# A gated-delta recursion, the samples' delta step and branch A's gates and state update as one stage behind the solve

## The chip, the cores and the metric

One core of one Trainium2 chip runs the whole kernel. The metric is the device time of one execution in microseconds (us), the median of the runs shown. The core has five engines with a program each: PE (matrix products), DVE (vector), ACT (scalar functions), POOL (GpSimd) and SP, which here only issues transfers. They wait for each other on semaphores.

## The reference, cut to what matters

The kernel is one step of a hybrid decoder layer for 512 prompt tokens and 8 sample tokens (one new token for each of 8 requests, each with a stored state): two token mixers on one input projection, then a retrieval of experts (PEER). The change touches mixer A only, the gated DeltaNet with 4 heads of 128 x 128 state:

```python
# prompt, chunked; T = inverse of (I + L) of each chunk; the kernel uses chunks of 128, so 4 of them
u = T @ (v * beta);  w = T @ (k * beta * exp(G))
def step(S, xs):                       # one chunk after the other
    v_new = u_c - w_c @ S
    o     = qg_c @ S + qk_c @ v_new
    S     = S * g_c + kd_c.T @ v_new
    return S, o
# samples: S_t = a (I - b k k^T) S_{t-1} + b k v^T,  o = S_t^T q    (a chunk of length 1)
o_a = rmsnorm(o_a, gn_a) * silu(gate_a)      # per head, for prompt and samples
```

The outputs of this part are the gated `o_a`, the last prompt state `delta_p` and the eight new sample states `delta_s`.

## The kernel before

The program is a row of stages. Each is a function under `@phase` (L166): it issues one block of five engine programs, and at its end all engines meet in a barrier (L173) before the next stage begins. A stage's SP program waits for its own transfers before that barrier. Within a stage the order of work on each engine is written out by hand; there is no planner.

Around the change the stages are these, in this order.

**convolve** (L788): the short convolution of the 12 channel tiles on DVE (L893 and L895), SiLU on ACT (L916), then the sums of squares for the L2 norm (ACT L926 squares, PE L855 products with a column of ones), then the transposes that make `k_tok` and `v_tok`.

**delta_prompt** (L945): it prepares the decay matrices, inverts the four triangular matrices by seven levels of doubling (L1018 to L1171; `n` counts the 28 pairs of level and chunk), and then, in the same block, does the rest for the prompt. PE makes `u` and `w` for each chunk (L1054 and L1055) into banks 2 and 3, ACT copies them to `X` and `LT` (L1111 and L1113), and PE waits for these copies before the next chunk. DVE multiplies `k_tok` by the decay (L1174). Then comes the recursion: for each chunk, PE makes `w S` (L1064), DVE subtracts it from `u` (L1180), PE makes the output and the state's increment interleaved (L1071 to L1073), and DVE scales `S` and adds the increment (L1183 and L1184); PE's next chunk waits for that. SP stores `delta_p` (L984).

**delta_sample** (L1269): SP loads the samples' states (four transfers of 512 KB, L1294), POOL clears `kq`, DVE fills it, PE multiplies all 32 old states by their keys and queries (L1348, 64 passes), and DVE works out the samples' new values and outputs in six operations of 8 x 512 (L1327 to L1333).

**gate_and_turn** (L1355): for the five token tiles (four of 128, one of 8), ACT squares and sums per head and takes the root (L1414 and L1417), DVE scales and gates (`scale`, L1387 and L1390), PE transposes (L1446), ACT writes the upper part (`upper`, L1421), DVE the rest (`lower`, L1397). Between them runs the update of the eight sample states (`StateUpdate`, L1191): for a sample, ACT masks the stacked keys (L1208), PE makes the outer products of four heads (L1218) into one of two banks, DVE adds them to the decayed states (L1229, four instructions). SP stores the states in pairs (L1238). `Stack` (L1243) makes the stacked rows: POOL clears, ACT copies twice, DVE subtracts (L1265).

A second thread of work runs through the stages. **Side** (L577) projects 24 column tiles of `w_in` for later use, a few in each stage, as filling for PE. A tile is loaded by SP (L601), rounded by ACT (L647), split by POOL (L621), multiplied by PE in two halves of 24 passes each (L635 to L637), taken out by ACT (`take`, L664) and stored by SP (L613). `SIDE_BESIDE` (L74) says how many tiles go beside which stage: 7 in convolve ("cv"), 10 in delta_prompt ("dp"), 1 in delta_sample ("ds"). In convolve, PE's program does all halves first and the sums of squares behind them; ACT takes a result after each channel tile's SiLU, and the squares follow after the last take.

Behind these stages come branch B's projection ("proj_b", whose first chunk of weights is loaded early into `raw0`), rotation, retention, the merge, the output projection, and the experts, which take more than half of the time.

The program that calls the stages (L2111) allocates `masks` and `conv_st` before the projection of A, and the states of the samples after delta_prompt.

## Time and profile before

| | us |
|---|---|
| median of 3 runs | 2331.44 (2331.11 to 2332.11) |
| the profiled execution | 2330.46 |
| its span in the trace | 2328.7 |
| PE busy over the span | 1856.2 (80%) |
| DVE busy | 1302.1 (56%) |
| ACT busy | 890.2 (38%) |
| POOL busy | 644.1 (28%) |
| granted TensorE clock, mean | 0.944 of full |

The span is measured from the first to the last recorded instruction; 1.8 us of the execution's time lie around it. Times in the rows are from the span's start. A busy PE is not PE at its peak, since products are pipelined. The shares are means over stages with different limits, so what a change in one stage is worth is read in that stage.

### The profile page before, as it was taken

To read this page: it belongs to the slowest core of one execution; us is meant where nothing else is said; L and a number is where in the kernel's file an instruction comes from. 1 tells how busy PE (TensorE), PEld (TensorE's weight loads), DVE (VectorE), ACT (ScalarE), POOL (GpSimd) and SP (SyncE) were. 2 spreads that over 40 slices of the span, in tenths; PEclk is the share of its full clock that TensorE was granted. 3 is DMA by queue.
4 is the path that set the end of the run, shared out by engine and by line. 5 is a ranking of instruction groups with operands and counts; after the bars stand their busy time and mean duration, and the time that the engine had idled before them with its cause. 6 is when DMAs were issued, how large, how long until landed. Compare 5 with 4: busy or idle time off the path is not lost.

```text
span 2328.7 us, 25982 instructions
## 1 busy us (share of the span) xinstructions
PE 1856.2 (80%) x8664; PEld 1192.2 (51%) x8664; DVE 1302.1 (56%) x2806; ACT 890.2 (38%) x2294; POOL 644.1 (28%) x558
## 2 busy tenths in 40 slices
PE   5989779737978788699997777777777877777776
PEld 4988679736975688555553232222322322222221
DVE  2136354322155451676775766767676876767664
ACT  4223212222223433344544444443544444444443
POOL 0002011000020000344444444444434444444442
PEclk9998789967998899799999999999999999999999
DMA  3312111026111532699999999999999999999996
GB/s 99 119 48 69 28 46 56 10 77 222 55 55 62 184 113 72 210 375 415 416 409 403 421 416 421 421 421 421 401 421 421 415 420 421 403 421 422 421 416 290
DMA packets 171783, 636.74 MB, mean 273 GB/s; under 512 B 12530, under 2 KB 97589, under 8 KB 104712
## 3 DMA queue, kind: packets, MB, share of 16 engines
q0 software_dynamic: 74880, 545.29, 56.8%
q1 hardware_dynamic: 96784, 89.98, 12.3%
q8 instruction: 60, 0.98, 0.2%
q14 instruction: 59, 0.48, 0.1%
HBM read 617.39 MB, written 17.93 MB: 273 GB/s over the span
## 4 chain that ended last, share of the span: by engine, by line
DMA 29%; PE 13%; DVE 8%; ACT 7%; issue 2%; POOL 0%; ACTq 0%; DVEq 0%
DMA ex_uv_row<-in_peer_uv,ex_eidx 28%; PE ps L1891 10%; DVE ex_uv_row L2054 4%; ACT L1937 2%; ACT ex_spread L1945 2%; ACT L1931 1%; ACT ret_tables L1942 1%; PE ps L571 1%; PE ps L572 1%; PE ps L573 1%; ACT ret_tables L1937 1%; DMA ex_uv_row<-in_peer_uv,ex_eidx_s 1%; DVE ex_sel L2026 0%; DVE ex_sel L2030 0%; DVE ex_best L2029 0%
## 5 line engine op out<-in xcount | busy, mean ns | idle before, releaser
L1891 PE MATMUL ps<-ex_uv_row,ex_spread 128*128 128x512 f32 (+1 forms) x2080 | 991.9, 612 | 258.1 <-ACT ex_spread L1945 252.9
L2054 DVE CUSTOM_DVE_ANT_0 ex_uv_row<-ex_uv_row,x_ffn 128x1024 f32<-128x1024 f32 x512 | 624.7, 1225 | 402.1 <-DMA ex_uv_row<-in_peer_uv,ex_eidx 397.2
L1891 PEld LDWEIGHTS ps<-ex_uv_row,ex_spread 128*128 128x128 f32 (+1 forms) x2080 | 364.5, 190 | 848.6 <-issue 848.4
L1853 POOL DMA_INDIRECT ex_uv_row<-in_peer_uv,ex_eidx x512 | 557.6, 1089 | 775.7 <-PE ps L1891 723.7
L1937 ACT ACTIVATE ret_tables<-ret_tables 128x1 f32<-128x1 f32 x520 | 104.7, 201 | 634.1 <-DVE ret_tables L2054 633.1
L1945 ACT ACTIVATE ex_spread<-square,ret_tables 128x128 f32<-128x128 f32 (+1 forms) x520 | 208.0, 400 | 17.0
L1942 ACT ACTIVATE ret_tables<-ret_tables 128x1 f32<-128x1 f32 x512 | 150.6, 294 | 16.8
L571 PE MATMUL ps<-proj_b_whi,x_lo 128*128 128x256 f32 (+1 forms) x320 | 90.5, 283 | 10.2 <-DVE proj_b_wlo L512 10.2
L571 PE MATMUL ps<-x_hi,ex_w_lo 128*128 128x260 f32 x256 | 84.8, 331 | 12.1 <-DVE ex_w_lo L1988 12.1
L573 PE MATMUL ps<-proj_b_whi,x_hi 128*128 128x256 f32 (+1 forms) x320 | 90.1, 282 | 0.0
L572 PE MATMUL ps<-proj_b_wlo,x_hi 128*128 128x256 f32 (+1 forms) x320 | 90.0, 281 | 0.0
L353 POOL TENSOR_TENSOR x_ffn<-norm_xn,norm_gains_row 128x1024 f32<-128x1024 f32 (+1 forms) x5 | 14.3, 2884 | 246.1 <-ACT norm_xn L303 246.1
L572 PE MATMUL ps<-x_lo,ex_w_hi 128*128 128x260 f32 x256 | 74.6, 291 | 0.0
L573 PE MATMUL ps<-x_hi,ex_w_hi 128*128 128x260 f32 x256 | 74.5, 291 | 0.0
L621 POOL TENSOR_TENSOR dp_w_lo<-dp_w_raw,dp_w_hi 128x1024 fp32r<-128x1024 f32 x10 | 23.9, 2397 | 173.6 <-ACT dp_w_hi L647 173.6
L571 PEld LDWEIGHTS ps<-proj_b_whi,x_lo 128*128 128x128 f32 (+1 forms) x320 | 54.4, 170 | 12.0 <-issue 10.2
L571 PE MATMUL ps<-x_hi,proj_a_wlo 128*128 128x260 f32 x192 | 55.0, 287 | 6.8 <-DVE proj_a_wlo L512 6.8
L571 PEld LDWEIGHTS ps<-x_hi,ex_w_lo 128*128 128x128 f32 x256 | 50.8, 198 | 18.1 <-DVE ex_w_lo L1988 12.4
L621 POOL TENSOR_TENSOR cv_w_lo<-cv_w_raw,cv_w_hi 128x1024 fp32r<-128x1024 f32 x7 | 18.4, 2629 | 146.6 <-ACT cv_w_hi L647 146.6
L573 PEld LDWEIGHTS ps<-proj_b_whi,x_hi 128*128 128x128 f32 (+1 forms) x320 | 54.5, 170 | 1.7
L572 PEld LDWEIGHTS ps<-proj_b_wlo,x_hi 128*128 128x128 f32 (+1 forms) x320 | 54.5, 170 | 1.7
L572 PE MATMUL ps<-x_lo,proj_a_whi 128*128 128x260 f32 x192 | 55.1, 287 | 0.0
(414 smaller groups left out, 3332.0 us busy)
## 6 DMA issues: line engine op xcount, KB each, us to landing
first_raw<-in_w_in SPq DMA_DIRECT2D x8, 1024.0 KB, 7.9
ex_uv_row<-in_peer_uv,ex_eidx POOLq DMA_INDIRECT x512, 12.5
dp_w_raw<-in_w_in SPq DMA_DIRECT2D x10, 512.0 KB, 4.1
proj_a_raw<-in_w_in SPq DMA_DIRECT2D x4, 1024.0 KB, 5.4
proj_b_raw<-in_w_in SPq DMA_DIRECT2D x4, 1024.0 KB, 5.3
S_sample<-in_state_ret SPq DMA_DIRECT2D x1, 4096.0 KB, 23.4
out_ret_s<-S_sample SPq DMA_DIRECT2D x4, 1024.0 KB, 4.5
q<-in_peer_wq SPq DMA_DIRECT2D x8, 512.0 KB
```

Of the source, the lines that this page charges most:

```text
L353: pool.tensor_tensor(keep[0][0:r, t, :], xn[0:r, t % 2, :], gains_row[0:r, :], ALU.mult).then_inc(kept, 1)
L571: pe.matmul(out, left(llo, c), right(rhi, c), start=(c == 0), stop=False)
L572: pe.matmul(out, left(lhi, c), right(rlo, c), start=False, stop=False)
L573: ins = pe.matmul(out, left(lhi, c), right(rhi, c), start=False, stop=(c == kc - 1))
L621: pool.tensor_tensor(self.w_lo[n % 2][:, :, :], self.raw[n % 2][:, :, :], self.w_hi[n % 2][:, :, :].bitcast(F32), ALU.subtract).then_inc(s ...
L1853: pool.indirect_dma_start(uv_row[:, n % RING, :], None, a["peer_uv"][0], bass.IndirectOffsetOnAxis(ap=index_of(n), axis=0)).then_inc(row_l ...
L1891: ins = pe.matmul(k.pv[t % 2][0:r, c, :], spread[:, n % RING, 0:r], uv_row[:, n % RING, D + c * 512:D + (c + 1) * 512], start=first, stop= ...
L1931: act.activation(gate[0:r, u, :], best[0:r, u, :], ACT.Exp, bias=shift[0:r, u:u + 1], accum_out=tot[0:r, u:u + 1]).then_inc(expd, 1)
L1937: fence(act, act.activation(c, c, ACT.Gelu), weighed, 2 * n + 1)
L1942: fence(act, act.activation(c, c, ACT.Copy, scale=gate_of(n)), weighed, 2 * n + 2)
L1945: act.activation(spread[:, n % RING, 0:what.shape[1]], what, ACT.Copy, scale=c).then_inc(spread_done, 1)
L2054: dve.tensor_tensor_reduce(u, u, x, 1.0, 0.0, ALU.mult, ALU.add, coef[:, n:n + 1]).then_inc(dotted, 1)
```

## The change

The block of delta_prompt is cut behind the solve: delta_solve ends with the inverses, and a new stage, delta_finish, does `u` and `w`, the recursion, the samples' step, the gates and the state update in one block with one barrier at its end. The tiles that pass from one to the other are allocated outside (`kept`); `masks` and `conv_st` are freed before delta_finish. The multiplication of `k_tok` moves into the solve's third level. The one Side tile of delta_sample moves to convolve, which now has 8. In the recursion the state has two buffers, its decay is made ahead, the state's increment is multiplied ahead of the output, and the samples' old-state products fill PE between them. The paired gathers of the experts stage are as they were.

```diff
-SIDE_BESIDE = {"ba": 2, "cv": 7, "dp": 10, "ds": 1, "gate_a": 0, "rope": 4, "rp": 0, "rs": 0, "gate_b": 0}
+SIDE_BESIDE = {"ba": 2, "cv": 8, "dp": 10, "rope": 4}
...
-def delta_prompt(k, a, o, pre, k_tok, v_tok, beta, logd, masks):
+def delta_solve(k, pre, k_tok, v_tok, beta, logd, masks, kept):
+    KEYS_AT = range(2 * NCH, 3 * NCH)
...
+                        if n in KEYS_AT:
+                            u = KEYS_AT.index(n)
+                            dve.wait_ge(dec_out, 2 * NCH + 2)
+                            dve.tensor_tensor(tok(k_tok, u), tok(k_tok, u), head_bc(kdg[:, u, :], P, P), ALU.mult).then_inc(kd_done, 1)
+                dve.wait_ge(kd_done, NCH)
+                dve.wait_ge(x_done, LEVELS * NCH)
...
+def delta_finish(k, a, o, pre, k_tok, v_tok, beta, logd, gate, kept, hi, lo, early):
...
+        sq, (qs, t1, dv) = XT[:, 0, :, :], (XT[0:NS, n, :, :].rearrange("p h e -> p (h e)") for n in range(1, NCH))
+        states = StateUpdate(k, "ds", S_sample, key_rows, key_of, value_rows, lambda b, h: spread_g[:, b, h:h + 1],
+                             o["delta_s"][0], (0, 2))
+        uw_banks = lambda t: (2, 3) if t % 2 == 0 else (0, 1)
+        turn_bank = lambda t: (7, 1)[t % 2]
...
             def _(sp):
                 for n in range(0, NS, 2):
+                    sp.dma_start(S_sample[:, n:n + 2, :, :].rearrange("p b h v -> p (b h) v"),
                                  a["state_delta"][0, n:n + 2].rearrange("b h k v -> k (b h) v")).then_inc(loaded[n // 2], 16)
+                begin(sp, early, early_loaded)
+                sp.wait_ge(s_done, NCH)
+                sp.dma_start(o["delta_p"][0, 0].rearrange("h k v -> k h v"), S[:, (NCH - 1) % 2, :, :]).then_inc(stored, 16)
+                states.on_sync(sp)
+                sp.wait_ge(stored, 16)
+                wait(sp, early_loaded, 16 * len(early))
...
+                pool.memset(kq[:, :, :, :], 0.0).then_inc(kq_cleared, 1)
+                key_stack.on_gpsimd(pool)
+                value_stack.on_gpsimd(pool)
...
+                def uw(t):
+                    wait(pe, uw_done, 2 * (t - 1))
+                    u_bank, w_bank = uw_banks(t)
...
+                def ws(t):
+                    pe.wait_ge(uw_done, 2 * t + 2)
+                    pe.wait_ge(s_done, t)
...
+                def kv(t):
+                    if t:
+                        pe.wait_ge(vn_done, t)
...
+                def old_states(h):
+                    pe.wait_ge(uw_done, 6)
+                    for b in range(NS):
+                        if h == 0 and b % 2 == 0:
+                            pe.wait_ge(loaded[b // 2], 16)
...
+                def turn(t):
+                    r = ROWS[t]
+                    pe.wait_ge(small_taken, 1)
+                    pe.wait_ge(ready, t + 1)
+                    wait(pe, lo_done, t - 1)
...
+                uw(0)
+                uw(1)
+                small_products()
+                uw(2)
+                kv(0)
+                out(0)
+                uw(3)
+                for t in range(1, NCH):
+                    ws(t)
+                    old_states(t - 1)
+                    kv(t)
+                    out(t)
+                    if t == NCH - 2:
+                        old_states(H - 1)
+                for t in range(NT):
+                    turn(t)
+                    if t == 1:
+                        pe.wait_ge(stacked, 2)
+                    if t:
+                        states.on_tensor(pe, t - 1)
+                for b in range(NT - 1, NS):
+                    states.on_tensor(pe, b)
...
+                def state(t):
+                    dve.wait_ge(kv_mm, t + 1)
+                    if t:
+                        ins = dve.tensor_tensor(S[:, t % 2, :, :], S_decayed[:, :, :], bank(6), ALU.add)
+                    else:
+                        ins = dve.tensor_copy(S[:, 0, :, :], bank(6))
+                    fence(dve, ins, s_done, t + 1)
+                    if t + 1 < NCH:
+                        own.fence(dve.tensor_tensor(S_decayed[:, :, :], S[:, t % 2, :, :], head_bc(gC[:, t + 1, :], P, P), ALU.mult))
...
+                key_stack.on_vector(dve, sample_keys).then_inc(stacked, 1)
+                state(0)
+                dve.wait_ge(small, 1)
...
+                for t in range(1, NCH):
+                    values(t)
+                    state(t)
+                    if t == NCH - 2:
+                        scale(0)
+                sample_step()
+                scale(1)
+                scale(2)
+                lower(0)
+                value_stack.on_vector(dve, dv).then_inc(stacked, 1)
+                scale(3)
+                lower(1)
+                states.on_vector(dve, 0)
+                scale(4)
+                lower(2)
+                states.on_vector(dve, 1)
+                lower(3)
+                states.on_vector(dve, 2)
+                lower(4)
+                for b in range(3, NS):
+                    states.on_vector(dve, b)
...
+                act.activation(eg[:, :], logd[0:NS, NT - 1, :], ACT.Exp).then_inc(e_done, 1)
+                key_stack.on_scalar(act, sample_keys)
+                act.wait_ge(cleared, 1)
+                for t in range(NCH - 1):
+                    uw_out(t)
+                out(0)
+                uw_out(NCH - 1)
+                for t in range(1, NCH):
+                    square(t - 1)
+                    out(t)
+                act.wait_ge(states_mm, 1)
+                act.activation(qs, k.pb[3][ROW_Q:ROW_Q + NS, :], ACT.Copy).then_inc(q_copied, 1)
+                square(NCH - 1)
+                upper(0)
+                act.wait_ge(dv_done, 1)
+                value_stack.on_scalar(act, dv)
+                act.wait_ge(stacked, 1)
+                states.on_scalar(act, 0)
+                states.on_scalar(act, 1)
+                upper(1)
+                act.wait_ge(sample_out, 1)
+                square(NCH)
+                for t in range(2, NT):
+                    states.on_scalar(act, t)
+                    upper(t)
+                for b in range(NT, NS):
+                    states.on_scalar(act, b)
...
+                    kept = [sb(n, [P, 4, H, P]) for n in ("LT", "X", "XT", "QK", "kbg")] + [sb("gC", [P, 4, H])]
...
+                        delta_solve(k, pre, k_tok, v_tok, beta, logd, masks, kept)
                     oa_hi, oa_lo = (k.sb(f"oa_{x}", [P, H, T], F32R, oa_ctx, "right") for x in ("hi", "lo"))
+                    delta_finish(k, a, o, pre, k_tok, v_tok, beta, logd, gate_a, kept, oa_hi, oa_lo,
+                                 [(raw0[:, :, :], first_chunk(w_in, COL_V_B))])
```

## Rows read from the trace of the kernel before

**Rows 1.** Stretches: length, busy PE, PEld, DVE, ACT, POOL (count), granted clock, DMA share, GB/s.

```profile
334.00:430.00 96.00, 95.35 (x830) 95.16 (x829) 41.27 (x64) 23.14 (x43) 14.13 (x6) 1.00 0.17 49
...
430.10:469.60 39.50, 22.57 (x176) 20.47 (x176) 9.28 (x14) 7.17 (x12) 0.00 (x0) 1.00 0.03 10
469.60:493.90 24.30, 9.05 (x58) 8.88 (x58) 1.45 (x10) 2.04 (x4) 3.50 (x2) 0.58 0.42 109
...
506.40:542.10 35.70, 12.46 (x52) 10.64 (x52) 19.25 (x65) 19.48 (x64) 0.98 (x2) 0.50 0.28 89
...
986.00:2328.70 1342.70, 1076.07 (x2827) 458.73 (x2825) 917.39 (x2183) 596.09 (x1763) 558.03 (x513) 0.99 0.99 409
```

**Rows 2.** Timeline of SP's queue at the stages' ends: start, us, what.

```profile
428.91 0.32 SPq L613 DMA_DIRECT2D side<-dp_result  x1
466.36 0.39 SPq L984 DMA_DIRECT2D out_delta_p<-S_delta  x1
469.67 4.18 SPq L1294 DMA_DIRECT2D S_ds<-in_state_delta  x4
```

**Rows 3.** DMA issues, 425 to 545 us: count, KB each, us to landing.

```profile
S_ds<-in_state_delta SPq DMA_DIRECT2D x4, 512.0 KB, 6.4
...
side<-dp_result SPq DMA_DIRECT2D x1, 260.0 KB, 2.0
...
out_delta_p<-S_delta SPq DMA_DIRECT2D x1, 256.0 KB, 2.3
```

**Rows 4.** Timelines of ACT, PE and DVE in the sample stage and the recursion.

```profile
481.33 1.06 ACT L647 ACTIVATE ds_w_hi<-ds_w_raw 128x1024 fp32r<-128x1024 f32 x1 [11.42 <-DMA ds_w_raw<-in_w_in]
...
493.95 7.18 PE L1348 MATMUL ps<-S_ds,ds_kq 128*40 128x128 f32 x64
...
451.56 0.69 DVE L1183 TENSOR_TENSOR S_delta<-S_delta,gC 128x512 f32<-128x512 f32 x1 [3.04 <-PE ps L1073]
...
501.24 0.68 DVE L1327 TENSOR_TENSOR ds_t<-ps,ds_eg 8x512 f32<-8x512 f32 x1 [7.00 <-PE ps L1348]
```

**Rows 5.** Groups of DVE instructions in the gates stage, 506.4 to 542.1 us.

```profile
L1229 DVE SCALAR_TENSOR_TENSOR S_ds<-S_ds,ds_spread_g,ps 128x128 f32<-128x128 f32 x32 | 8.6, 342 | 0.0
L1390 DVE SCALAR_TENSOR_TENSOR v_tok<-v_tok,gate_a_ss,gate_a 128x128 f32<-128x128 f32 (+1 forms) x20 | 5.7, 346 | 0.2
L1397 DVE SCALAR_TENSOR_TENSOR oa_lo<-ps,vecs,oa_hi 128x512 fp32r<-128x512 f32 (+1 forms) x5 | 3.2, 650 | 5.8 <-ACT oa_hi L1421 5.8
L1387 DVE RECIPROCAL gate_a_ss<-gate_a_ss 128x4 f32<-128x4 f32 (+1 forms) x5 | 0.9, 173 | 3.8 <-ACT gate_a_ss L1417 3.8
```

**Rows 6.** Timelines of PE, DVE and ACT at the gates stage's end.

```profile
532.60 2.12 PE L1218 MATMUL ps<-gate_a_value_rows,gate_a_key_of 72*128 72x128 f32 x8 [2.69 <-DVE S_ds L1229]
...
535.76 2.15 DVE L1229 SCALAR_TENSOR_TENSOR S_ds<-S_ds,ds_spread_g,ps 128x128 f32<-128x128 f32 x8
...
542.10 2.19 ACT L495 ACTIVATE proj_b_whi<-first_raw 128x512 fp32r<-128x512 f32 x4 [6.53 <-PEq L173]
```

**Rows 7.** Timelines of DVE, POOL, ACT and PE in the convolution.

```profile
200.75 2.33 DVE L895 SCALAR_TENSOR_TENSOR conv_taps<-pre,vecs,conv_taps 128x512 f32<-128x512 f32 x3
...
203.51 4.33 DVE L895 SCALAR_TENSOR_TENSOR conv_taps<-pre,vecs,conv_taps 128x512 f32<-128x512 f32 x3
...
204.77 2.53 POOL L621 TENSOR_TENSOR cv_w_lo<-cv_w_raw,cv_w_hi 128x1024 fp32r<-128x1024 f32 x1 [5.00 <-ACT cv_w_hi L647]
...
211.18 0.37 ACT L664 ACTIVATE cv_result<-ps 128x260 f32<-128x260 f32 x1
...
217.28 1.16 ACT L926 ACTIVATE l_sq<-pre 128x520 f32<-128x520 f32 x2
...
217.97 15.43 PE L855 MATMUL ps<-square,l_sq 128*128 128x1 f32 x80 [3.06 <-ACT l_sq L926]
```

**Rows 8.** PE and its granted clock (the 0.50) in the sums of squares.

```profile
217.90:233.30 15.40, 15.33 (x80) 0.50 0.05 17
```

**Rows 9.** One group of DVE instructions in the solve, 305 to 430 us.

```profile
L1163 DVE TENSOR_TENSOR XT<-XT,ps 128x512 f32<-128x512 f32 x20 | 13.8, 689 | 54.4 <-PE ps L1044 54.4
```

More of the change, by code:

```diff
@@ new lines, in scale @@
+                def scale(t):
+                    r = ROWS[t]
+                    dve.wait_ge(rooted, t + 1)
+                    own.fence(dve.reciprocal(ss[0:r, t, :], ss[0:r, t, :]))
+                    for h in range(H):
+                        e = slice(h * P, (h + 1) * P)
+                        ins = dve.scalar_tensor_tensor(v_tok[0:r, t, e], v_tok[0:r, t, e], ss[0:r, t, h:h + 1],
+                                                       gate[0:r, t, e], ALU.mult, ALU.mult)
+                    ins.then_inc(ready, 1)
@@ L1316, in _ @@
+                dve.wait_ge(kq_cleared, 1)
                 for h in range(H):
@@ L1331, in _ @@
-                dve.wait_ge(q_copied, 1)
-                own.fence(dve.tensor_tensor(heads(qs), heads(qs), head_bc(eg[:, :], NS, P), ALU.mult))
-                own.fence(dve.tensor_tensor(v[0:NS, :], qs[0:NS, :], t1[0:NS, :], ALU.add))
-            @block.tensor
-            def _(pe):
-                side.quarters(pe, 2 * side.halves)
-                pe.wait_ge(ready, 1)
-                for h in range(H):
-                    pe.matmul(k.pb[2][0:NS, h:h + 1], prod[:, h, :], k.ones[:, 0:1], start=True, stop=True)
-                pe.wait_ge(spread, 1)
-                pe.matmul(k.pb[0][:, 0:BH], k.ones[0:NS, :], gs[:, :, :].rearrange("p b h -> p (b h)"),
-                          start=True, stop=True).then_inc(g_sum, 1)
-                for h in range(H):
-                    for b in range(NS):
-                        if h == 0 and b % 2 == 0:
-                            pe.wait_ge(loaded[b // 2], 16)
-                        ins = pe.matmul(k.pb[1][0:ROW_Q + NS, h * P:(h + 1) * P], kq[:, h, b, :], S[:, b, h, :],
-                                        start=(b == 0), stop=(b == NS - 1))
-                ins.then_inc(states, 1)
@@ L1411, in _, with uw_out, out, square @@
             def _(act):
-                def square(t, r):
+                def uw_out(t):
+                    act.wait_ge(uw_mm, t + 1)
+                    for x, n in zip((X, LT), uw_banks(t)):
+                        ins = act.activation(x[:, t, :, :], bank(n), ACT.Copy).then_inc(uw_done, 1)
+                    act.wait_ge(uw_done, 2 * t + 2)
+                def out(t):
+                    act.wait_ge(o_mm, t + 1)
+                    fence(act, act.activation(tok(v_tok, t), bank(5), ACT.Copy), o_done, t + 1)
+                def square(t):
+                    r = ROWS[t]
                     for h in range(H):
-                        ins = act.activation(sq[0:r, h, :], heads(o_tok, t, r)[:, h, :], ACT.Square, scale=width ** -0.5,
+                        ins = act.activation(sq[0:r, h, :], v_tok[0:r, t, h * P:(h + 1) * P], ACT.Square, scale=P ** -0.5,
                                              accum_out=ss[0:r, t, h:h + 1])
@@ L1425, in _ @@
-                value_stack.on_scalar(act, dv[0:NS, :])
+                    act.activation(hi[:, :, t * P:t * P + r], bank(turn_bank(t))[:, :, 0:r], ACT.Copy,
+                                   scale=k.gn_a).then_inc(hi_done, 1)
+                act.activation(eg[:, :], logd[0:NS, NT - 1, :], ACT.Exp).then_inc(e_done, 1)
+                key_stack.on_scalar(act, sample_keys)
                 act.wait_ge(cleared, 1)
-                square(0, ROWS[0])
-                act.wait_ge(stacked, 2)
+                for t in range(NCH - 1):
+                    uw_out(t)
```

289 lines of the change are left out of this document (100 added, 189 removed).

## The prediction

> **What bounds the kernel now.** I read the busy time by stretches first, since the kernel is a row of stages with a barrier after each: what counts is where a stage's engines all stand still. The experts stage, from 986 us on, has its DMA engines busy 0.99 of the time [rows 1]; nothing here touches it, so time saved ahead of it stays saved. The dense part of the solve is PE's: 95.4 of the 96 us from 334 on, at full clock, side products filling every gap. The three stretches that the change rebuilds are bound by no engine. Recursion: PE 22.6 of 39.5 us. Sample stage up to its state products: PE 9.1 of 24.3, and all of that for one side tile. Gates: PE 12.5, DVE 19.3, ACT 19.5 of 35.7 [rows 1]. With the samples' products and values between them (493.9 to 506.4) it is 112 us of one engine waiting for another.
>
> Then the timelines say for what. In the recursion DVE waits 3.04 us for a group that holds output and increment interleaved, though it needs only the increment [rows 4]. In the sample stage ACT waits 11.42 us for the side tile's weights, behind 2 MB of states; then come rounding, split and two halves before PE begins the samples' state products at 493.95, 24 us into the stage [rows 2, 4]. In the gates stage DVE lacks work for nearly half of the time while PE waits 2.69 us for DVE's update: two engines alternating [rows 1, 6].
>
> **The new stage, part by part.** All in the old trace's clock.
>
> Its start. The solve's last side result is issued at 428.91 and lands 2.0 us later [rows 2, 3]. A boundary costs 1.0 us: 466.36 plus 2.3 of landing is 468.7, and the next stage begins at 469.67. So it starts at 431.9, called 0 below. PE began this work at 430.1 before; the cut costs 1.8 us.
>
> PE's queue up to the last output. Passes are 0.112 us apart: 64 in 7.18 us, at full clock [rows 4]. u and w take 64 passes (two for each product of 128x128), the small products 10, w S 24, the increments 32, the outputs 56, the old states 64: 250 passes, 28.0 us. Are there gaps? The second u, w pair has banks of its own, and the third waits for ACT's copies for some 0.2 us, because ACT first stacks the keys. In a chunk w S (0.9), old states (1.8), increment (0.9) and output (1.8) follow each other. DVE's vn is there about 2.0 us after w S began (0.9 of issue, 0.4 of drain and signal, 0.69), ahead of the 2.7 at which the increment wants it; the new state likewise stands 2.0 us after the increment began, against 2.7. The removed decay step (0.69) is made in that cover. So PE runs through, to 28.0; the third state's increment ends its issue at 26.0, and DVE has the last state at 27.0 (0.4 of drain and signal, 0.69 for the addition [rows 4]).
>
> States loaded. The last of four loads was issued about 3 us into the stage and such a load lands in 6.4 [rows 2, 3]: about 9.6. PE wants the first pair at 10.7 and the last at 12. Cost nothing, cover 2 us; if a load is late, the increment, the output and every later chunk stand behind it in PE's queue. The early chunk for proj_b (1 MB) is now queued behind the states; it is needed only at the stage's end. The store of delta_p goes out behind both, in cover.
>
> POOL clears kq and the two row tiles first: 1.2 and 2 times 0.5 us, and PE asks for kq only after 3.6 us.
>
> DVE's queue behind the recursion. From 27.0: six operations of 8x512 at 0.68 and 0.03 between them, 4.2 [rows 4]; four scales, 4/5 of 5.7 and of 0.9, 5.3; all lowers 3.2; the value stack 0.7; eight updates 8.6 [rows 5]. That is 22.0, to 49.0. The first scale is done in the recursion. For the last updates PE needs 1.06 us for one sample's products (2.12 for two [rows 6]) against DVE's 1.08; with two banks I allow 0.4 of waiting: 49.4. Is ACT later? Its queue after the last output copy is under 17 us (squares 2 x 1.6, uppers 3.0, masks 5.7, stacks 1.3, copy 1.2, and short waits), so it is the shorter one.
>
> Its end. The last update ended at 537.91 and proj_b began at 542.10: 4.2 us for store and barrier [rows 6]. So proj_b begins at 431.9 + 49.4 + 4.2 = 485.5 in place of 542.1: **56.6 us saved**. The side tile with its waits, two boundaries, the recursion's waits and the alternation of the gates are all in this one number.
>
> **What moves elsewhere.** The k_tok multiplications go into the solve: 4 of 0.69 us. The cover is DVE's waiting there, 54.4 us in 20 places, 2.7 each [rows 9]. I take nothing; bound up to 2 us if POOL's splits fall on them, nothing below, since the four left no path that bounded before.
>
> The side tile in convolve is the price. Count halves and takes from 0; halves 14 and 15 are new. The take of half 11 begins at 211.18 [rows 7]; ACT must now round the new tile ahead of it (1.06 [rows 4]), so it ends at 212.6, and half 13, which needs its bank and else began at about 211.8, starts at 212.8. A half has 24 passes of 0.12 us (95.35 us for 830 recorded ones, and some wider than the mean [rows 1]), 2.9; so half 14 could start at 215.7 and half 15 at 218.5. Now POOL. A channel tile's three taps take 2.33 us, but 4.33 where POOL's split starts beside them [rows 7], 2.0 more; the new split, 2.53 us from 212.3 on, falls on the last two channel tiles. Then the last SiLU comes at 218.2, the take of half 13 at 218.8, half 15 at 219.2 and its take at 222.6; the first square follows at 223.0 and not at 217.28 [rows 7]: **5.7 us lost**. Without the delay of DVE it would be 4.8. The Trainium skill (SBUF — State Buffer, "Who interferes with whom") says that a DVE instruction with two SBUF inputs contends with a GpSimd instruction that reads SBUF, not with one that only writes it. By that rule the taps are delayed, as the trace shows, and the sum is 5.7; by a rule without contention it would be 4.8. The same rule leaves the clearing of tiles in the new stage free.
>
> Bounds of this price: the sums of squares run at the low level (granted clock 0.50, 1.2 GHz; 80 passes in 15.4 us [rows 7, 8]) after PE idled 3.1 us. PE now idles some 1 us there. At 0.112 a pass they would need 9.0, so up to 6.4 may come back; I take none, since one-column products look idle to whatever fell there. The other way, two halves at 1.2 GHz instead of 2.4 cost 5.8 more.
>
> **Sum.** 56.6 - 5.7 = 50.9. The profiled execution took 2330.46, so 2279.6; the median stands 0.98 above it: **2280.5**.
>
> **Rivals.** (a) The alternation stays: PE, ACT and DVE in the tail still hand over one by one, as between 516 and 536 us. Then the tail takes the old stage's pace, 22.0 of work plus the 5.8 and 3.8 that DVE waited for ACT before [rows 5], less what the longer start covers, 7.5 more: **2288**. For it: the same helpers with two banks, and PE's 2.69 [rows 6]. Against: the updates now stand behind scales and lowers that feed others. (b) The clock holds in convolve: 6.4 less, **2274**. For: the shorter idle. Against: above. (c) Slower: the solve loses its clock. Its 96 dense us were granted 1.00, 2.4 GHz [rows 1]; at 1.2 GHz they would be 192, so 2280.5 + 96 = **2376**. The place is the dense part of the solve, whose start shifts by 5.7 us and whose DVE gets four instructions more; it decides once more than 51 us of the 96 are granted 1.2 GHz. Against it: the level rose there and held for the whole stretch. (d) The stage does not end earlier: something unmoved, like the early load of 1 MB or a state load, holds it. A load that is 3 us late moves the whole by 3 us (2283); to give back all, **2331**, it would have to be 50 us late, and in the old stage even the side weights behind 2 MB of states had landed 12 us in [rows 2, 4].
>
> **How the numbers follow.** Forecast 0.76, (a) 0.10, (b) 0.09, (c) 0.025, (d) 0.025. A measurement of this kernel tells 0.2% from no change, 4.7 us; forecast, (a) and (b) are all far beyond it: faster 0.95. (d) is the same, and (c) with part of (d)'s mishaps slower. The range takes in (a) and (b): from 2280.5 - 6.4 - 2 (PE at full clock in the updates) = 2272 to 2280.5 + 7.5 + 2 + 1 = 2291.
>
> **What would show it.** The stretch from the last XT update to proj_b's first rounding should be about 56 us instead of 112, with PE nearly without a gap for 28 us, and DVE without a wait above 1 us from the last state on. Convolve's first square should come about 5.7 us later, with one more tap group of 4.3 us. The solve should have its length. The forecast is wrong if PE in the chunks waits for DVE or a load, if DVE's tail shows the old waits for ACT, or if the stages behind change their length.

## The result, and the profile after

The changed kernel takes **2278.31 us** (median of 4 runs, 2275.99 to 2279.18), the kernel before beside it 2331.78 (2331.11 to 2334.23): a ratio of 0.9769, with a 95% interval of 0.9757 to 0.978. 2280.5 was forecast. The profiled execution of the changed kernel took 2275.99, its span is 2274.1.

The marks in the table divide that span. The first square is ACT's first for the L2 norm; the copy of G (the summed log decays) is the solve's first DVE instruction; "last XT" is the end of the last XT update; "states" the end of the last state update of the samples; proj_b begins with its first rounding.

```
us from the start        first square   copy of G   last XT   states   proj_b   behind it   span
before                        217.28      256.38     430.07    537.91   542.10    1786.6    2328.7
changed                       222.87      258.81     432.20    483.85   488.14    1786.0    2274.1
changed, second profile       224.43      261.69     434.00    485.64   489.94    1786.4    2276.3
```

From last XT to proj_b it was 112.03 us and is 55.94: **56.1 saved**. Ahead of it 2.1 are lost, behind it 0.6 won, and 56.1 - 2.1 + 0.6 is the 54.6 by which the span fell. The new stage itself, by its stretches (length, busy PE, PEld, DVE, ACT, POOL, granted clock, DMA share, GB/s; compare the three of [rows 1]):

```profile
434.00:462.10 28.10, 28.00 (x243) 26.59 (x244) 10.67 (x30) 13.61 (x42) 2.09 (x3) 1.00 0.41 114
462.10:483.90 21.80, 12.83 (x61) 11.18 (x59) 21.08 (x64) 13.83 (x35) 0.00 (x0) 0.60 0.28 80
```

First PE is the bound for 28 us, at full clock and without a gap, then DVE for 21.8, of which it is busy 21.1; the second part, from DVE's last state of the recursion to its last update of a sample state, is called the tail below. Where the old three stretches had one engine waiting for another, the stage now passes its bound over once. The timeline of DVE and ACT (start, us, what; in brackets the idle time before it and what ended that):

```profile
431.51 0.69 DVE L1112 TENSOR_TENSOR XT<-XT,ps 128x512 f32<-128x512 f32 x1 [2.53 <-PE ps L1029]
434.13 0.19 DVE L1397 TENSOR_TENSOR df_prod<-pre 128x32 f32<-128x32 f32 x1 [1.93 <-PEq L173]
...
454.32 0.69 DVE L1363 TENSOR_TENSOR df_S_decayed<-df_S,gC 128x512 f32<-128x512 f32 x1
...
461.31 0.69 DVE L1358 TENSOR_TENSOR df_S<-df_S_decayed,ps 128x512 f32<-128x512 f32 x1 [2.27 <-PE ps L1290]
462.03 0.68 DVE L1372 TENSOR_TENSOR XT<-ps,df_eg 8x512 f32<-8x512 f32 x1
...
477.96 5.89 DVE L1170 SCALAR_TENSOR_TENSOR df_S_sample<-df_S_sample,df_spread_g,ps 128x128 f32<-128x128 f32 x20
...
488.14 2.19 ACT L495 ACTIVATE proj_b_whi<-first_raw 128x512 fp32r<-128x512 f32 x4 [7.08 <-PEq L173]
```

Between 462.03 and 483.85 no instruction of DVE has an idle time in brackets; the last five of eight updates stand in one group of 20. The wait for the output (3.04 us in [rows 4]) is now one of 2.27 for the increment, and it costs PE nothing: PE issues the rest of the samples' state products and the increment itself meanwhile. The old stages' DVE groups [rows 5] have nearly the same busy time and no longer wait for ACT:

```profile
L1170 DVE SCALAR_TENSOR_TENSOR df_S_sample<-df_S_sample,df_spread_g,ps 128x128 f32<-128x128 f32 x32 | 8.9, 337 | 0.3
L1386 DVE SCALAR_TENSOR_TENSOR v_tok<-v_tok,df_ss,gate_a 128x128 f32<-128x128 f32 (+1 forms) x20 | 5.7, 344 | 0.2
L1393 DVE SCALAR_TENSOR_TENSOR oa_lo<-ps,vecs,oa_hi 128x512 fp32r<-128x512 f32 (+1 forms) x5 | 3.2, 637 | 0.0
```

Between the solve's work and proj_b there are now two barriers, where there were three. SP's queue at the first of them, from the issue of the solve's last side result to the first load of states (compare [rows 2]):

```profile
431.03 0.32 SPq L613 DMA_DIRECT2D side<-dp_result  x1
434.06 4.73 SPq L1252 DMA_DIRECT2D df_S_sample<-in_state_delta  x4
```

In the convolution the extra side tile stands where it was expected (timelines of DVE, POOL, ACT and PE; [rows 7] are their counterparts):

```profile
208.38 2.33 DVE L895 SCALAR_TENSOR_TENSOR conv_taps<-pre,vecs,conv_taps 128x512 f32<-128x512 f32 x3
...
211.14 4.34 DVE L895 SCALAR_TENSOR_TENSOR conv_taps<-pre,vecs,conv_taps 128x512 f32<-128x512 f32 x3
...
212.40 2.53 POOL L621 TENSOR_TENSOR cv_w_lo<-cv_w_raw,cv_w_hi 128x1024 fp32r<-128x1024 f32 x1 [5.00 <-ACT cv_w_hi L647]
...
222.59 0.39 ACT L664 ACTIVATE cv_result<-ps 128x260 f32<-128x260 f32 x1 [2.43 <-PE ps L637]
222.87 1.15 ACT L926 ACTIVATE l_sq<-pre 128x520 f32<-128x520 f32 x2
...
223.55 12.26 PE L855 MATMUL ps<-square,l_sq 128*128 128x1 f32 x80 [1.00 <-ACT l_sq L926]
```

The first square comes 5.59 us later (5.7 forecast). But the 80 passes behind it took 12.26 us instead of 15.43, and PE idled 1.00 us ahead of them and not 3.06. So the copy of G comes only 2.43 us later.

### The profile page after: what moved, and what is told of

Read it like the earlier page. It is cut to its first block, busy times and chain, and to the rows that moved or that the text cites. A ratio compares the mean times of both kernels' runs of the same rounds, so it can differ in the third digit from the quotient of the medians.

```text
span 2274.1 us, 25972 instructions
## 1 busy us (share of the span) xinstructions
PE 1841.2 (81%) x8664; PEld 1184.0 (52%) x8664; DVE 1303.4 (57%) x2807; ACT 889.5 (39%) x2294; POOL 639.1 (28%) x558
## 4 chain that ended last, share of the span: by engine, by line
DMA 30%; PE 13%; DVE 8%; ACT 7%; issue 2%; POOL 0%; ACTq 0%; DVEq 0%
DMA ex_uv_row<-in_peer_uv,ex_eidx 30%; PE ps L1930 10%; DVE ex_uv_row L2093 4%; ACT L1976 2%; ACT ex_spread L1984 2%; ACT L1970 1%; ACT ret_tables L1981 1%; PE ps L571 1%; PE ps L573 1%; PE ps L572 1%; ACT ret_tables L1976 1%; DMA ex_uv_row<-in_peer_uv,ex_eidx_s 1%; DVE ex_sel L2065 0%; DVE ex_sel L2069 0%; DVE ex_best L2068 0%
```

## The experiments

Each was run 4 or 5 times beside the kernel before, in four groups. The kernel before took 2331.39 us in the first (side_only, tile_in_solve, nine_tiles, states_behind), 2329.51 in the second (output_first, one_bank, early_scale, tile_in_tail), 2331.13 in the third (changed_again, tile_only, scale_only) and 2333.79 in the fourth (tail_again); a median moves by up to 4 us from group to group, so small effects are read from the length of a stretch in the traces and not from the medians. Each ratio is to the kernel before of its own group; of the variants of the changed kernel below, only one_bank's interval lies clear of the changed kernel's (0.9757 to 0.978).

**1. Only the side tile, in the old kernel (side_only).**

```diff
-SIDE_BESIDE = {"ba": 2, "cv": 7, "dp": 10, "ds": 1, ...
+SIDE_BESIDE = {"ba": 2, "cv": 8, "dp": 10, "ds": 0, ...
```

> The kernel before, with the one side tile moved from the sample stage to the convolution and nothing else. Theory A (each stage's end is set by a chain of waits, as walked in the prediction): the samples' state products no longer start at 493.95 but when the last of the four state loads has landed, near 480; 48 of their 64 passes are then still to do, at 1.2 GHz since PE was idle, so the sample stage shrinks by 11 to 16 us, and the convolution grows by what it grew in the changed kernel, 2.9. Sum 8 to 13 us faster than before, about 2321. Rival B (the side tile was nearly the whole gain, the merging little): the sample stage shrinks by 24 us or more and most of the 54 us is there, about 2290. Rival C (the tile's path was hidden by the state loads anyway): no change beyond the convolution, about 2334.

2321.61 us, ratio 0.9963 (0.9949 to 0.9977). The tile's move alone brings 9.8 us. The old sample and gates stages, from their first DVE instruction to the last update, fall from 68.19 to 55.08, 13.1 less, and the last XT update comes 3.5 later. PE now begins the state products when the first states have landed, and not behind the side tile (493.95 in [rows 4]); it waits for the loads in four places, 4.0 us in all:

```profile
479.85 1.07 PE L1348 MATMUL ps<-S_ds,ds_kq 128*40 128x128 f32 x4 [2.05 <-DMA S_ds<-in_state_delta]
```

From the last XT update to proj_b it is 100.2 us and was 112.0, 11.8 less, since the recursion between them took 1.3 us more in this trace (its granted clock was 0.50 for 3.4 us of it). So of the 56 us 12 to 13 are the tile's, and the other 43 to 44 come from running the recursion, the sample step, the gates and the update as one. How these divide among the barriers and the engines' waits was not measured; runs 4 to 6 each undo one ordering inside the new stage.

**2. The tile in the solve instead of the convolution (tile_in_solve).**

```diff
-... "cv": 8, "dp": 10 ...
+... "cv": 7, "dp": 11 ...
...
-side.quarters(pe, 2 if n < 3 * NCH else 1)
+side.quarters(pe, 2 if n < 4 * NCH else 1)
...
-if n < 2 * NCH or n % 2 == 0:      # ACT takes a result
+if n < 3 * NCH or n % 2 == 0:
```

> The changed kernel with 7 tiles beside the convolution and 11 in the solve (four more quarters of a tile in the solve's fourth level). Theory A (the solve is bound by PE's passes from its second level on): 48 passes at 0.115 us make the solve 5.5 us longer, the convolution gets back 2.9 us; net 2.6 us slower than the changed kernel. Rival D (the solve has room beside its chain of products, and the convolution is the worse place): the solve grows by under 1 us, net 2 to 5 us faster.

2281.40 us, ratio 0.9786 (0.9772 to 0.9799). The solve from the copy of G to the last XT update takes 179.87, the first square is back at 218.25, the copy of G at 257.37. The four other traces with seven tiles in the convolution have 173.6 to 174.0, so it is some 6.1 us for two halves of 24 passes, 5.8 at 0.12: in the solve the tile costs its full length, since that stretch is PE's [rows 1]. The last XT update comes at 437.24, 3.8 later than in the mean of the traces with eight tiles in the convolution (433.43), so by the traces the convolution was the cheaper place.

**3. Nine tiles in the convolution (nine_tiles).**

```diff
-... "cv": 8, "dp": 10 ...
+... "cv": 9, "dp": 9 ...
...
-side.quarters(pe, 2 if n < 3 * NCH else 1)
+side.quarters(pe, 2 if n < 2 * NCH else 1)
...
-if n < 2 * NCH or n % 2 == 0:      # ACT takes a result
+if n < NCH or n % 2 == 0:
```

> The changed kernel with 9 tiles beside the convolution and 9 in the solve. Theory A with what the trace of the changed kernel showed (the tile delayed the first square by 5.6 us, and 2.7 us came back because PE's clock fell only after four of the eight groups of sums): the first square comes another 5.8 us later, up to 3 us more come back if the clock falls later still, and the solve is 5.5 us shorter: between 3 us faster and no change. Rival D: the solve does not get shorter and the total is 3 to 6 us slower. If the give-back was chance, the convolution grows by the full 5.8.

2279.65 us, ratio 0.9781 (0.9768 to 0.9794). The ninth tile puts the first square at 230.07, 7.2 us later than in the changed kernel, and shortens the solve by 5.6 (to 167.75). From the first square to the copy of G it is 37.95, where eight tiles have 35.9 to 37.3 and seven 39.1: the ninth gives nothing further back. The copy of G, at 268.02, is 7.3 later than in the mean of eight tiles (260.69), more than the 5.8 that was expected at most. A gain over eight is not there.

**4. The samples' state products behind the chunks (states_behind).**

```diff
                 for t in range(1, NCH):
                     ws(t)
-                    old_states(t - 1)
                     kv(t)
                     out(t)
-                    if t == NCH - 2:
-                        old_states(H - 1)
+                for h in range(H):
+                    old_states(h)
```

> The changed kernel with all 64 passes on the samples' old states issued behind the last chunk's output instead of between the chunks. Theory A (they fill PE where it would wait for vn, and the tail hangs on DVE's queue behind the last state and the samples' step): a chunk needs 4.7 us instead of 5.6, so the last state comes about 4 us earlier, but the samples' step must wait for the 7.2 us of products behind it and starts 3.5 us later; stage and kernel 3.5 us slower. Rival E (the recursion alone sets the stage's end): 4 us faster.

2280.21 us, ratio 0.9783 (0.9768 to 0.9797); the stage from its first DVE instruction to the last update 53.02 us instead of 49.72, 3.3 more (3.5 expected). PE now stands still ahead of each increment:

```profile
447.31 1.16 PE L1290 MATMUL ps<-df_vn,k_tok 128*128 128x128 f32 x8 [0.85 <-DVE df_vn L1366]
```

So the 16 state products in each chunk cover DVE's vn, as the prediction had it. Without them there is a wait of 0.81 to 0.85 in each of the three chunks; the last state comes 4.9 us earlier, but the work that had filled the chunks follows behind it, and the samples' step waits for that.

**5. The output ahead of the increment (output_first).**

```diff
                     old_states(t - 1)
+                    pe.wait_ge(vn_done, t)
+                    out(t)
                     kv(t)
-                    out(t)
```

> The changed kernel with each chunk's output multiplied ahead of the state's increment. Theory A: the increment's result then has no products behind it that hide the drain and the addition, so PE idles 1.1 us before the second chunk (before the third the old states of the fourth head hide it), and the last state comes 1.8 us later: the last state is 2.9 us later and the stage as much longer. Rival F (the addition was hidden anyway): under 0.5 us.

2280.26 us, ratio 0.9783 (0.9768 to 0.9798), the stage 52.62 us, 2.9 more, as expected. The state is late, and the next w S waits for it, in this one place (timelines of DVE and PE):

```profile
450.76 0.69 DVE L1359 TENSOR_TENSOR df_S<-df_S_decayed,ps 128x512 f32<-128x512 f32 x1 [3.98 <-PE ps L1290]
...
451.59 1.13 PE L1281 MATMUL ps<-df_S,LT 128*128 128x128 f32 x8 [0.87 <-DVE df_S L1359]
```

**6. One bank for the outer products (one_bank).**

```diff
-... o["delta_s"][0], (0, 2))
+... o["delta_s"][0], (0,))
```

> The changed kernel with the sample states' outer products in one bank instead of two. Theory A (the last five updates are bound by DVE, 1.18 us each, only because PE works one ahead): they become PE 1.06, DVE 1.08 and 0.4 of hand-over, 2.5 each, five times 1.3 = 6.6 us more, and up to 1 more among the first three. Rival G (PE and ACT already alternate with DVE there): under 2 us.

2283.74 us, ratio 0.9802 (0.9787 to 0.9817), the stage 56.41 us, 6.7 more. DVE's eight updates wait for PE, and PE for them (the group, from 463 us on, and the last update in DVE's timeline):

```profile
L1170 DVE SCALAR_TENSOR_TENSOR df_S_sample<-df_S_sample,df_spread_g,ps 128x128 f32<-128x128 f32 x32 | 9.0, 341 | 6.8 <-PE ps L1159 6.8
```

```profile
490.82 1.12 DVE L1170 SCALAR_TENSOR_TENSOR df_S_sample<-df_S_sample,df_spread_g,ps 128x128 f32<-128x128 f32 x4 [1.27 <-PE ps L1159]
```

That is the alternation of rival (a), brought about by the one bank. With two banks the same group waits 0.3 us in all.

**7 and 8. The second scale ahead of the last state, and the last states stored one by one (early_scale); then also the side tile in the new stage's tail (tile_in_tail).**

```diff
                     values(t)
+                    if t == NCH - 1:
+                        scale(1)
                     state(t)
                     ...
                 sample_step()
-                scale(1)
...
-                states.on_sync(sp)              # SP's program
+                for n, w in ((0, 2), (2, 2), (4, 2), (6, 1), (7, 1)):
+                    sp.wait_ge(states.updated, n + w)
+                    sp.dma_start(...)
...
```

> The changed kernel with two edits to the tail: the scaling of the second token tile is put between the last chunk's vn and its state, where DVE waits 2.27 us, and the last pair of sample states is stored one by one. Theory A (DVE's queue behind the last state sets the end, then the store of the last piece): 1.25 us from the scale and about 1.0 from a last store of 256 KB instead of 512 (the 256 KB one of the prompt's state landed in 2.3): 2.2 us faster. Rival G (ACT's chain of squares and upper parts sets the tail): the scale gives nothing, and 1.0 remains.

2276.12 us, ratio 0.9764 (0.9751 to 0.9777). From the end of the last state to the last update it is 20.6 us, where the changed kernel has 21.85: the scale's 1.25. The last store has half the size, and from the last update to proj_b it is 3.76 and not 4.29: 0.5, half of what was expected of the store. In run 8, with the same stores, it is 3.82, and in run 12 4.23, so this gain is not a steady one. The stage as a whole is not shorter (50.09), since the last state came 1.6 later. Run 10 shows by what.

For the tile in the tail the raw weights and the result use the memory of kbg, which is no longer needed by then; PE takes three quarters of the tile behind the first transposition, and one behind the second.

> The kernel with the early scale and the single stores, and the side tile moved from the convolution into the new stage: loaded once u and w are made, rounded and split during the recursion, multiplied by PE between the transposes of the first two token tiles, where PE waits 4.2 us for DVE. Theory A (PE is idle there, and DVE sets the tail): the convolution gets its 2.9 us back and the tail grows by at most 1.5, since POOL's split falls on the recursion and the second transposes come up to 1.5 us later: 1.5 to 3 us faster than early_scale, 4 to 5 faster than the changed kernel. Rival H (the split by POOL blocks DVE inside the recursion, or the two takes push ACT onto the path): no gain over early_scale.

2272.59 us, ratio 0.9756 (0.9743 to 0.9769). The first square is at 217.38, the copy of G at 256.51 and last XT at 430.09, as before the change. The tail is 20.6 us and the last state comes 29.5 after the stage's first DVE instruction, both as in early_scale without the tile, which therefore costs nothing there. Its stage took 50.09 us, because the first products were again slow (last section).

**9. The changed kernel once more (changed_again).** No edit.

> The changed kernel itself, unaltered, beside the two below on the same chip. Expected within 1.5 us of its first median (2278.3 us where the kernel before takes 2331.8). The trace is wanted for the clock: if the price of the convolution's eighth side tile depends on the clock and not on the code, the copy of G ends here anywhere between 258.8 and 261.3 us, as over the six earlier traces with eight tiles (the first trace had 258.8).

2276.75 us (2275.8 to 2281.66), ratio 0.9768 (0.9755 to 0.9782), 1.6 us under the first median. The stage is 49.72 us long, like the first time. The copy of G stands at 261.69, 0.4 behind the expected range and 2.9 later than in the first profile, from the same code: a first square 1.6 later, then 14.64 us and not 12.26 for the 80 passes of the sums, but 21.94 instead of 22.99 from their end to the copy of G. The solve took 172.31 instead of 173.39.

**10. Only the tile in the tail (tile_only).** Run 8 without the scale and the stores of run 7.

> One half of the best kernel so far (-5.7 us against the changed one): the eighth side tile goes from the convolution to the new stage's tail, the scale and the stores stay as in the change. Theory (the tile is free in the tail, and costs 2.4 to 4.9 us in the convolution, 3.7 on the mean): 3.7 us less than the changed kernel (2.4 to 4.9); copy of G at 256.4 to 257.4 us; the new stage from its first DVE instruction to the last update 49.7 us, as in the changed kernel, +-0.4. Rival (the tile found room only because the scale had gone ahead): the tail grows by what the tile holds the shared engines, POOL's split of 2.4 us beside DVE or the passes, so the stage takes 51 to 52 us and the whole wins 1 to 2 us only.

2277.00 us, ratio 0.9771 (0.9757 to 0.9784): the same as the changed kernel, where 3.7 us less was expected. The copy of G is at 257.65, 0.25 behind the expected range, and last XT at 431.59, 1.8 ahead of the mean of the traces with eight tiles. The stage took 51.35 us, the number of the rival, but not for its reason: from the end of the last state to the last update it is 21.85 us, exactly the changed kernel's. The 1.6 are lost in the stage's first products. Two rows of PE's timeline, then the stretch of the stage's first 3.6 us (its granted clock is the 0.56):

```profile
433.49 0.46 PE L1284 MATMUL ps<-v_tok,XT 128*128 128x128 f32 x2 [2.63 <-PEq L173]
...
434.96 0.63 PE L1284 MATMUL ps<-v_tok,XT 128*128 128x128 f32 x2
```

```profile
433.50:437.10 3.60, 3.60 (x19) 3.60 (x19) 2.13 (x12) 1.55 (x4) 2.04 (x3) 0.56 0.61 171
```

and the same stretch in changed_again:

```profile
435.90:439.50 3.60, 3.60 (x32) 3.60 (x32) 2.13 (x12) 2.12 (x5) 2.04 (x3) 1.00 0.60 170
```

19 passes against 32: most of the stretch at 1.2 GHz in the one, all of it at 2.4 in the other. early_scale has 18 passes at 0.57 there, and its last state comes as late (29.5 us after the first DVE instruction in both, 27.87 in the changed kernel), so the 1.6 us are the clock's and not the edit's; run 11 has early_scale's order of work at full clock.

**11. Only the second scale earlier (scale_only).** The first hunk of run 7.

> The other half: the second scale stands ahead of DVE's last wait for a state, nothing else is changed (four stores of 512 KB). Theory (DVE's queue behind the last state sets the end, so 1.25 us of work taken out of it shortens the stage by that): from the end of the last state's addition to the last update 20.6 us instead of 21.85, and 1.3 us less than the changed kernel in the whole; where the first products of the stage are granted less than full clock, the last state comes up to 1.6 us later and cancels it in that run. Rival (the scale delays what PE waits for, so that nothing is won whatever the clock): the last state later by about 1 us also where the first products run at full clock, and the whole the same as the changed kernel within 0.3.

2276.09 us, ratio 0.9761 (0.9748 to 0.9774). Here the first products ran at full clock, and the stage took 48.46 us, 1.26 less than the changed kernel's, with 20.59 from the last state on. The last state came no later than in the changed kernel (27.87 after the first DVE instruction in both): the theory holds, the rival falls. In DVE's timeline the scale now stands in the wait for the increment, of which 1.01 us is left:

```profile
460.60 1.14 DVE L1386 SCALAR_TENSOR_TENSOR v_tok<-v_tok,df_ss,gate_a 128x128 f32<-128x128 f32 x4
462.75 0.69 DVE L1358 TENSOR_TENSOR df_S<-df_S_decayed,ps 128x512 f32<-128x512 f32 x1 [1.01 <-PE ps L1290]
```

**12. Run 8 once more (tail_again).** No edit.

> The kernel with the tile in the tail, the early scale and the last states stored one by one, a second time, since its first median (2272.6 us, with 2329.5 for the kernel before) came from another call than the two runs of the changed kernel (2278.3 and 2276.8, with 2331.8 and 2331.1), and its two halves alone brought 0 and 1 us. If its parts add up as the traces say (2.9 us for the tile at the solve's end, 1.25 for the scale, 0.5 for the stores, less 1.6 where the stage's first products are granted the low clock), it stands 3 to 5 us under the changed kernel: ratio to the kernel before 0.975 to 0.976. If the first median was luck: 0.9765 or above.

2280.01 us (2275.03 to 2280.65), ratio 0.9771 (0.9756 to 0.9786): above the 0.9765 at which the first median was to be called luck. In its profile last XT is at 430.94 and proj_b at 487.20, against 432.20 and 488.14 in the first profile of the changed kernel and 434.00 and 489.94 in the second. So it is 1 to 3 us ahead there, but the stages behind proj_b's start, with the same code, took 1791.3 us and not 1786. **No variant is shown to beat the changed kernel.** The one part that a trace shows to pay is the scale, 1.26 us in its stretch, less than these medians can tell.

## Why the prediction was right, and where it was off

**Sign and size.** 2280.5 was forecast, 2278.3 measured, within the range; the mechanism was the forecast one: PE's queue without a gap, then DVE's. One term, the side tile's price, was put too high; it is named below.

**The start.** 1.8 us for the cut, worked out from the landing and the boundary: the new stage's first product begins 1.90 us after last XT (434.10 against 432.20), and the last store of the solve is issued 3.03 us before SP's first load of the stage, against 2.0 + 1.0.

**PE's queue, 28.0 us without gaps.** 28.00 busy of 28.10. The outputs are issued until 28.8 us into it, 0.8 more than 250 passes at 0.112 make, as the first product of a group stands some 0.1 us further from its neighbour than the others. So DVE has the last state at 27.9 and not 27.0.

**DVE's queue behind it, 22.0 + 0.4.** 21.85. The chosen 0.4 of waiting for two banks was 0.3 in all, four gaps of 0.07 to 0.08 between the last five updates; with these gaps the five took 1.18 each (5.89) against the 1.08 that was put in, and the work ahead of them took 16.0 against 16.6. Runs 6 and 11 show that this queue sets the end: 6.7 us of waits put into it come out at proj_b, 1.25 of work taken out of it come off. Together with the point above, the stage to its last update is 49.75 from the first product, 49.4 forecast: a miss of 0.9 us and one of 0.55 the other way, so that the total is nearer than its parts by luck.

**The covers.** Costs of nothing were claimed for vn, the decay step and the state loads. Run 4 removes vn's cover and gets the wait for it back in each chunk; run 5 removes the cover of the new state and gets one wait of 0.87 us and a later increment in every chunk. The decay step's cover shows in run 8: one such step took 1.59 us there and not 0.69, and the last state came no later than in early_scale. The state loads were there in time: no product in the chunks waits for one. Four k_tok multiplications in the solve: side_only, which has the old solve, took 172.34 us for it, and the five traces of the new solve whose sums of squares ahead took as long (14.6 us) took 172.2 to 172.4, so they cost 0.1 us at most.

**The side tile in the convolution, 5.7 us lost.** This is the term that was mis-sized. To the first square it is right: 5.59 in this trace, and 5.9 as a mean (217.87 over five traces with seven tiles, 223.75 over eight with eight). Behind it the prediction held the sums of squares to their old 15.43 us ("I take none") and gave the solve its old length; both gave something back. At the copy of G the tile costs 2.4 in this trace and 3.7 as a mean (256.98 and 260.69), at the last XT update 2.1 and 2.8 (430.67 over four traces with seven tiles and ten in the solve, 433.43 over eight). From the first square to the last XT update it is 212.7 to 213.1 us in those four, and with eight tiles 209.3 to 209.7 in seven traces and 210.6 in one (early_scale). So some 3.3 us come back nearly every time, but not always in the same place: in the changed kernel's first trace 3.2 of them lie in the sums; in the six traces whose sums took 14.6 us, 0.8 lie in the sums, 1.0 between the sums and the copy of G, and about 1.4 in the solve. In the side_only trace the granted clock of that stretch reads:

```profile
224.60:238.50 13.90, 13.87 (x76) 13.57 (x77) 0.00 (x0) 5.61 (x8) 0.00 (x0) 0.54 0.06 20
```

and in the changed kernel's

```profile
223.50:235.80 12.30, 12.25 (x81) 11.91 (x81) 0.00 (x0) 5.62 (x8) 0.00 (x0) 0.67 0.06 23
```

against the 0.50 of [rows 8]. Rival (b), the clock that holds, came true in part: 3.2 of its 6.4 us in the changed kernel's profile, 0.8 in side_only's. A granted clock between 0.50 and 1.00 is part of the stretch at 1.2 GHz and part at 2.4: where PE came to the sums after 1.0 us of idle it ran a part of them at 2.4 (the granted clock was 1.00 for their first 4.2 us in the changed kernel's first trace and for 1.0 in its second), and after 3.0 us none (15.43 us in tile_in_solve too). That the shorter idle is the reason was not tried apart from the tile, and the reason that the prediction gives for taking none was tried by no run: all have the same 80 products there.

**The contention.** The new tap group of 4.34 us stands beside POOL's split at 212.40, and the one ahead of it, without a split, takes 2.33. By the prediction's working this makes 5.7 of 4.8; the last SiLU and the take behind it come at 218.27 and 218.81, where it had them at 218.2 and 218.8, but no run has the tile without a split beside the taps. Run 8 shows the same at a second place (POOL and DVE in the timeline):

```profile
452.54 2.36 POOL L626 TENSOR_TENSOR ds_w_lo<-kbg,ds_w_hi 128x1024 fp32r<-128x1024 f32 x1 [18.49 <-ACT ds_w_hi L652]
...
453.13 0.69 DVE L1377 TENSOR_TENSOR df_S<-df_S_decayed,ps 128x512 f32<-128x512 f32 x1 [2.20 <-PE ps L1305]
453.85 1.59 DVE L1382 TENSOR_TENSOR df_S_decayed<-df_S,gC 128x512 f32<-128x512 f32 x1
```

Both begin inside the split. The first, with one input in PSUM, keeps its 0.69 us; the second, with two in SBUF, takes 1.59, where the changed kernel's takes 0.69 (the row at 454.32 above). The Trainium skill (SBUF — State Buffer, "Who interferes with whom") says that a DVE instruction with two SBUF inputs contends with a GpSimd instruction that reads SBUF, and that one with at most one SBUF input, outside its 2-port modes, does not. The trace agrees with both.

**The rivals.** (a), the alternation, is absent: 0.3 us of waiting in the updates, and run 6 shows what it would have looked like. (c), the solve losing its clock, is absent: its dense part reads

```profile
338.20:431.50 93.30, 93.27 (x812) 93.08 (x810) 41.24 (x63) 21.64 (x42) 14.16 (x6) 1.00 0.17 49
```

with the granted clock at 1.00. (d), an unmoved load, is absent: from the last update to proj_b it is 4.29 us, where it was 4.18 before.

**What is left of the difference.** The step that was off is the side tile's price: by its own terms the prediction lost 5.7 in front where 2.1 were lost, 3.6 too much; it saved 56.6 where 56.1 were saved, 0.5 too much; and 0.6 came behind. That is 3.6 - 0.5 + 0.6 = 3.7 for the profiled execution (2279.6 forecast, 2275.99 measured). The median moved less, 53.5 us against 50.9 forecast.

## What to carry to other kernels

Where consecutive stages are each one engine waiting for another, add up each engine's own work in the joined stage and look for the one queue that stays full at each time: here PE's 28 us and then DVE's 22 gave the new length to within half a microsecond (each part to within one), while the waits that went away did not have to be priced one by one. The order within it matters by what it covers: put the product that the next step waits for ahead of the one that nobody waits for, and independent work into the gap behind it. And PE work put ahead of a stretch that was granted the low clock may cost less than its length: here the first square came 5.9 us later and the last XT update 2.8, so such a stretch's duration is not to be taken as fixed.

## What had not been expected of the hardware

**The same idle, another clock.** At the new stage's start PE idles 2.6 us. In five profiles the first 3.6 us of the stage were then granted 0.55 to 0.60 (early_scale, tile_in_tail, tile_only, tail_again, nine_tiles), in the other seven that have this stage, the changed kernel's two among them, 1.00; the last state comes 1.4 to 1.6 us later for it. early_scale and scale_only have the same program up to there, the same idle (2.64 and 2.63) and last XT at 433.62 and 433.63, and one is granted 0.57 and the other 1.00. They differ in what went before: early_scale's 80 passes of the sums took 12.34 us and scale_only's 14.64, and in the solve the granted clock rose to 1.00 for good at 326.8 and at 317.9. Over the twelve profiles it had risen 103 to 109 us before the stage's first product in the five, and 115 to 118 in the seven. Whether that decides it was not tried. The three profiles with the tile in the tail are all among the five: of what they won ahead of the stage, 2.6 us on the mean, they lost 1.6 again in it.

**The same code, up to 7 us apart.** The stages from proj_b on took 1784.5 to 1791.3 us over all profiles, with the same code. One of the places is the branch B stage, where two successive lowers stand 10.91 us apart in the changed kernel's first profile (DVE's timeline)

```profile
695.87 1.40 DVE L1668 SCALAR_TENSOR_TENSOR x_lo<-ps,vecs,x_hi 128x512 fp32r<-128x512 f32 x2
...
706.78 1.40 DVE L1668 SCALAR_TENSOR_TENSOR x_lo<-ps,vecs,x_hi 128x512 fp32r<-128x512 f32 x2
```

and 9.70 in its second (698.16 and 707.86). Effects of 1 or 2 us were therefore visible only in the stretch in which they arose.
